# The experts' second product: two passes in place of three for a last block of at most 64 tokens

## What is computed

```python
def _clamped_swiglu(hgu):
    x_glu = jnp.minimum(hgu[..., ::2], SWIGLU_LIMIT)
    x_lin = jnp.clip(hgu[..., 1::2], -SWIGLU_LIMIT, SWIGLU_LIMIT)
    return x_glu * jax.nn.sigmoid(SWIGLU_ALPHA * x_glu) * (x_lin + 1.0)
...
    group_sizes = jnp.bincount(flat_e, length=N_EXPERTS).astype(jnp.int32)
    xs = h[tok]
    hgu = lax.ragged_dot(xs, w_gate_up, group_sizes) + b_gate_up[e_sorted]
    act = _clamped_swiglu(hgu)
    out = lax.ragged_dot(act, w_down, group_sizes) + b_down[e_sorted]
    out = out * gates.reshape(-1)[order][:, None]
    return jax.ops.segment_sum(out, tok, num_segments=L)
```

## Time and profile before

| | us |
|---|---|
| median of 3 executions | 5597.11 |
| lowest and highest | 5595.68 and 5604.63 |
| the profiled execution, its own time | 5600.18 |
| its span in the profile | 5598.8 |
| PE busy / weight loads busy | 5331.9 (95%) / 4757.0 (85%) |
| DVE / ACT / POOL busy | 3565.4 (64%) / 2642.7 (47%) / 614.2 (11%) |
| mean granted clock of TensorE | 0.979 |

### The profile page before, as it was taken

The page is one execution under the profiler, slowest core; times in us unless marked ns, Lnnn a source line. Parts: engine busy times, 40 slices in busy tenths (PEclk is TensorE's granted clock), DMA queues, the critical chain, the costliest instruction groups (busy, mean ns, idle before and its releaser), DMA issues. The chain is left out here.

```text
span 5598.8 us, 92579 instructions
## 1 busy us (share of the span) xinstructions
PE 5331.9 (95%) x30192; PEld 4757.0 (85%) x30193; DVE 3565.4 (64%) x6848; ACT 2642.7 (47%) x5266; POOL 614.2 (11%) x545
## 2 busy tenths in 40 slices
PE   8999979899799999998979999999999999999994
PEld 7777868788799999997869999999899888888894
DVE  6667758533566667776764655655667745577776
ACT  3444331333455556665433534533546534366665
POOL 1101100133000000000220100110101100011113
PEclk9999999999899999999989999999999999999997
DMA  4332335455411101201534744554557644467667
GB/s 145 112 114 92 109 126 166 124 145 152 147 61 59 37 24 61 78 9 57 167 106 132 243 139 166 192 180 146 193 195 234 235 131 157 146 223 246 244 236 251
DMA packets 260439, 809.25 MB, mean 145 GB/s; under 512 B 22305, under 2 KB 168449, under 8 KB 224513
## 3 DMA queue, kind: packets, MB, share of 16 engines
q1 hardware_dynamic: 230352, 717.05, 36.6%
q0 software_dynamic: 27536, 84.88, 6.7%
q10 hardware_dynamic: 2336, 4.45, 0.2%
HBM read 662.84 MB, written 143.47 MB: 144 GB/s over the span
## 5 line engine op out<-in xcount | busy, mean ns | idle before, releaser
L2721 DVE TENSOR_TENSOR e_wl<-r_raw,e_wh 128x1024 fp32r<-128x1024 f32 x770 | 930.1, 1222 | 435.2 <-DVEq L2343 431.8
L2637 ACT CAST e_wh<-r_raw 128x1024 fp32r (+1 forms) x770 | 790.9, 1043 | 864.2 <-ACTq L2343 841.9
L2570 PE MATMUL ps<-e_hT,e_wl 128*128 128x192 f32 (+5 forms) x4096 | 1196.3, 292 | 0.0
L2563 PE MATMUL ps<-e_hT,e_wh 128*128 128x384 f32 (+2 forms) x2560 | 797.2, 374 | 6.1 <-PEq L2343 4.3
L2570 PEld LDWEIGHTS ps<-e_hT,e_wl 128*128 128x128 f32 x4096 | 776.1, 189 | 10.7
L2565 PE MATMUL ps<-e_hT,e_wh 128*128 128x352 f32 (+2 forms) x1536 | 529.4, 345 | 9.0 <-PEq L2343 9.0
L2569 PE MATMUL ps<-e_hT,e_wh 128*128 128x352 f32 (+2 forms) x1536 | 527.2, 343 | 0.0
L2563 PEld LDWEIGHTS ps<-e_hT,e_wh 128*128 128x128 f32 x2560 | 480.3, 188 | 51.6 <-issue 10.7
L2591 PE MATMUL ps<-e_wh,e_aTh 128*128 128x512 f32 x1248 | 504.5, 404 | 5.2 <-PEq L2343 5.2
L1777 ACT CAST a_PT<-ps 128x512 fp32r<-128x512 f32 x512 | 288.0, 589 | 464.7 <-PE ps L1717 464.7
L1732 PE MATMUL ps<-a_PT,a_V 128*128 128x256 f32 (+1 forms) x3264 | 504.3, 294 | 0.2 <-DVE a_sc L1820 0.2
(11 more groups left out here) (367 smaller groups left out, 9329.6 us busy)
## 6 DMA issues: line engine op xcount, KB each, us to landing
r_raw<-in_wgu SPq DMA_DIRECT2D x130, 2048.0 KB
r_raw<-in_wdn SPq DMA_DIRECT2D x64, 2048.0 KB
m_raw<-in_w SPq DMA_DIRECT2D x56, 1024.0 KB, 4.8
qTd<-p_qt SPq DMA_DIRECT2D x32, 640.0 KB, 6.6
e_bd<-in_bdn SPq DMA_DIRECT2D x32, 512.0 KB, 3.8
kTd<-p_kt SPq DMA_DIRECT2D x32, 448.0 KB, 4.3
a_Q<-qTd SPq DMA_DIRECT2D x7, 2048.0 KB, 9.2
a_V<-vd SPq DMA_DIRECT2D x24, 512.0 KB, 4.5
```

The costliest lines, as they stand in the source:

```text
L2563: t = pe.matmul(both, wh, E.hT[:, :, k, 0:v], start=(k == 0), stop=False)
L2570: t = pe.matmul(p[:, 0:v], wl, E.hT[:, 0, k, 0:v], start=False, stop=(k == 7))
L2637: act.copy(E.wh[:, h, x], raw[:, 2048 * h + 1024 * i:2048 * h + 1024 * i + 1024]).then_inc(E.hi_full, 1)
L2721: return dve.tensor_tensor(lo, src, hi.bitcast(F32), ALU.subtract)
```

## The change

`down` is split in two functions. `first` is block 0: its three passes as before, with the low activation's pass ahead of the low weights' one. `later` is a block b >= 1, which now goes pass by pass (4 matmuls of `aTh` by `wh`, 4 of `aTl` by `wh`, 4 of `aTh` by `wl`); the middle pass stands under a branch and is left out when the group's tokens m are at most 128 b + 64, that is, when this is the last block and has at most 64 tokens. For such a group DVE copies the low parts of the last block's first 64 tokens (`aTl`) into the free columns 64 to 127 of that block in `aTh` (`pair`, behind the whole loop of `gate_up` and ahead of the bias), so that one pass over `wh` makes both products, the low one in rows 64 to 127 of the PSUM bank. `outcome` then adds those rows to the first 64 with a second instruction. In every group, short last block or not, PE takes the new semaphore `paired` between block 0 of the stretch (4, 0) and its block 1, and DVE raises it behind the place of the copy. In `outcome` of every block b >= 1 the first instruction is now linked, and `out_full` is raised by a queue instruction behind the branch.

```diff
-    def down(c, h, b, rn):
-        g = product_bank(c, b)
+    def part(g, h, b, k, x, y, start, stop):
+        return pe.matmul(E.G[g][:, :], x[:, 4 * h + k, b * 128:(b + 1) * 128], y[:, h, k * 512:(k + 1) * 512],
+                         start=start, stop=stop)
+
+    def first(c, h, rn):
+        b, g = 0, product_bank(c, 0)
...
-            for m, (x, y) in enumerate(((E.aTh, E.wh), (E.aTh, E.wl), (E.aTl, E.wh))):
...
+            for m, (x, y) in enumerate(((E.aTh, E.wh), (E.aTl, E.wh), (E.aTh, E.wl))):
+                t = part(g, h, b, k, x, y, h == k == m == 0, h == 1 and k == 3 and m == 2)
...
+    def later(c, h, b, rows_here):
+        g = product_bank(c, b)
+        if h == 0:
+            take(pe, E.g_free[g])
+        for k in range(4):
+            part(g, h, b, k, E.aTh, E.wh, h == k == 0, False)
+        with pe.If(rows_here > paired(b)):
+            for k in range(4):
+                part(g, h, b, k, E.aTl, E.wh, False, False)
+        for k in range(4):
+            t = part(g, h, b, k, E.aTh, E.wl, False, h == 1 and k == 3)
+        if h:
+            t.then_inc(E.g_full[g], 1)
...
-            for b in range(4):
-                with present(pe, r, b):
-                    down(c, h, b, rn)
+            first(c, h, rn)
+            if (c, h) == (4, 0):
+                take(pe, E.paired)
+            for b in range(1, 4):
+                with pe.If(r > b):
+                    later(c, h, b, m)
...
+        t = dve.scalar_tensor_tensor(out=E.Y[:, b, cols], in0=E.G[g][:, :], scalar=1.0 / SWIGLU_ALPHA, in1=E.bd[:, cols],
+                                     op0=ALU.mult, op1=ALU.add)
+        if b == 0:
+            t.then_inc(E.out_full[b], 1)
+        else:
+            link(t)
+            with dve.If(rows_here <= paired(b)):
+                link(dve.scalar_tensor_tensor(out=E.Y[0:64, b, cols], in0=E.G[g][64:128, :], scalar=1.0 / SWIGLU_ALPHA,
+                                              in1=E.Y[0:64, b, cols], op0=ALU.mult, op1=ALU.add))
+            dve.sem_inc(E.out_full[b], 1)
         over(E.g_free[g])
...
+    def pair(blocks, rows_here):
+        with dve.If(dve.snap(blocks * 128 + rows_here * -1, min_val=0, max_val=512) >= 64):
+            over(E.dv)
+            take(dve, E.dv)
+            at = dve.snap(blocks * 128 - 128, min_val=0, max_val=384)
+            link(dve.tensor_copy(E.aTh[:, :, bass.ds(at + 64, 64)], E.aTl[:, :, bass.ds(at, 64)]))
+        dve.sem_inc(E.paired, 1)
...
         by_width(dve, m, gate_up, TAKEN)
+        pair(r, m)
         bias()
```

More of the change, by code:

```diff
@@ L2336, in experts_stage @@
     E.own_in, E.own_full, E.summed = sem("own_in"), sem("own_full"), sem("summed")
-    E.dv, E.warmed = sem("dv"), sem("warmed")
+    E.dv, E.warmed, E.paired = sem("dv"), sem("warmed"), sem("paired")
     return E
@@ L2361, with paired @@
 BOTH = 256
+def paired(b):
+    return 128 * b + 64
 def by_width(eng, m, program, widths):
@@ L2596, in down @@
             t.then_inc(E.g_full[g], 1)
+    def later(c, h, b, rows_here):
[11 more added lines that the diff above has]
+            t.then_inc(E.g_full[g], 1)
     ahead = Ahead(E, pe, "pe")
-    first, _, _ = ahead.group()
+    r0, _, _ = ahead.group()
     for b in range(4):
-        with present(pe, first, b):
+        with present(pe, r0, b):
             rows(b, 0)
@@ L2711, in link @@
         take(dve, E.dv)
-    cell = {s: i for i, s in enumerate([E.raw_free] + E.hT_full + E.hx_free + E.g_free + [E.bd_free])}
+    cell = {s: i for i, s in enumerate([E.raw_free] + E.hT_full + E.hx_free + E.g_free + [E.bd_free, E.dv])}
     def over(s):
@@ L2778, in gate_up, with outcome @@
             dve.reg_mov(slot, now * -1 + 1)
-    def outcome(c, b):
+    def outcome(c, b, rows_here):
         g = product_bank(c, b)
@@ L2808, in experts_dve @@
     with groups(E, dve) as q:
-        left = dve.snap(was, min_val=0, max_val=4)
+        left, left_rows = dve.snap(was, min_val=0, max_val=4), dve.snap(was_rows, min_val=0, max_val=512)
         r, rn, m = ahead.group()
@@ L2812, in experts_dve @@
             with dve.If(left > b):
-                outcome(5, b)
+                outcome(5, b, left_rows)
         over(E.bd_free)
@@ L2825, in experts_dve @@
             with present(dve, r, b):
-                outcome(4, b)
+                outcome(4, b, m)
         for i in range(2):
@@ L2834, in experts_dve @@
         dve.reg_mov(was, r)
+        dve.reg_mov(was_rows, m)
         ahead.move()
-    left = dve.snap(was, min_val=0, max_val=4)
+    left, left_rows = dve.snap(was, min_val=0, max_val=4), dve.snap(was_rows, min_val=0, max_val=512)
     for b in range(4):
         with dve.If(left > b):
-            outcome(5, b)
+            outcome(5, b, left_rows)
 def norm_stage(nc, A, banks, sumd, out, eps, since, ctx):
```

20 lines of the change are left out of this document (9 added, 11 removed).

## The result

| | before | after |
|---|---|---|
| median of the runs | 5596.4 us (4 runs, 5595.44 to 5604.63) | 5802.46 us (4 runs, 5799.17 to 5807.29) |
| profiled execution, its span | 5600.2 us (time) | 5799.17 us, span 5797.8 us |
| experts' stage | 2588 us | 2790 us |
| passes of `aTl` over `wh` | 1248 | 1040 |

The ratio is 1.0366, with an interval of 1.0348 to 1.0383: 206 us slower. The direction was forecast, the size was not; 5802 lies far above the range of 5616 to 5670.

What follows compares the result with a forecast made beforehand. PE was taken to bound the experts' stage, busy for 2569.5 of 2588 us. The terms -47.2 + 36.2 + 45.9 + 4 + 6 + 1 gave +46 us, so 5643 us as median, range 5616 to 5670.

Steps and rivals of the forecast that it cites:

- the links on DVE in other places fall in its idle time: DVE's queue in the experts' stage: the other added links cost nothing, as DVE is idle for 37% of the stage.
- cost nothing by themselves: PE's queue: splitting blocks into passes and the new order in `first` add 0 us, as the queue runs ahead.
- a rival at 0.12: TensorE's clock falls in the new pauses: 7 x 3.4 = 24 us more, 5667 us; chance 0.12.
- the price of a pass: PE's second product: 16 matmuls of 0.227 us saved in each of 13 short-ended groups, 47.2 us.
- the new wait: PE ahead of block 1 of (4, 0): 36.2 us added in 16 long-ended groups, 45.9 in the short-ended ones.
- 4 + 1 us beside them: 4 us for one-block groups waiting for `paired`, 1 us for the longer sum at the last group's end.
- saving and paying come out even: The 13 short-ended groups come out nearly even: 47.2 us saved, 45.9 paid.
- the longer sum: `outcome(5, last)` delays ACT's scale, the next weights and PE's second unit in the following group: 6 us (2 to 10).
- Hidden or cheap: Rival: PE's new wait is hidden or cheap, so the kernel gets faster; near 5580 us needs 1 us pauses; chance 0.03.
- even (0.05): Rival: time within 0.2% (11 us), with pauses of 1.6 and 2.6 us and no cost in successors; chance 0.05.
- pass not skipped: Rival: the branch fails to skip the pass or the copy lies elsewhere, only costs left, +93, 5690 us; chance 0.02.
- PE's idle time in the stage: Sign on PE's timeline: idle time in the experts' stage near 110 us instead of 18.5.

Runs made afterwards that it cites:

- after_lean: The changed kernel with width 432 left out of the forms on DVE and ACT, so DVE's loop has 309 instructions; 5686.79 us (1.0156).
- filled: after_lean with eight matmuls that nobody reads, run by PE into a free bank ahead of each take of `paired`; 5652.52 us (1.0094).
- hybrid_act: late_pair with ACT's order of experiment 6, and all four stretches in two passes where the short block is third or fourth; 5578.51 us (0.9965).
- after_shift: The changed kernel, DVE's loop left at 359 instructions, with 80 never-run memsets under a branch ahead of that loop; 5683.34 us (1.0149).
- before_lean: The kernel before with width 432 left out of the forms on DVE and ACT, so DVE's loop has 264 instructions; 5597.97 us (0.9994).
- experiment 6: ACT makes the next group's first pair of high weights ahead of the scale: on late_pair 5588.36 us (0.9982), on before_lean 5600.9 us (1.0004).
- late_pair: after_lean with two passes only in the last two stretches (c = 5), copies made later, behind low weights; 5587.47 us (0.9977) against the kernel before.

## Why the prediction was wrong

**Where it failed: the code.** The step is the pair of sentences that "the links on DVE in other places fall in its idle time" and that the split and the new order "cost nothing by themselves". No term of the sum, and no rival, asked what 45 more instructions in DVE's loop do by being there: the code stood at nothing without a reason. DVE was idle for 37% of the stage, and that hid what they execute, but not their loading, most of which comes at the one place where DVE is on the path, the start of a group. Measured in the changed kernel itself, by moving it: 119 us of the 206, of which some 40 are the clock behind the pauses that the loading makes. That alone puts it outside the range. The question could have been asked blind, since the stage before loads next to no code (6 packets) and the size of the loop can be counted; the price could not, as no row of the kernel before shows a reload.

**Where it failed in part: the clock.** This was a rival at 0.12, worked out at 24 us for the seven longest pauses alone. It happened, and in more places: 22 times in the second products of the changed kernel and in 17 of 32 pauses of `after_lean`, after idle times from 2.03 us up, when I had taken one pause of 3.1 us without a fall as evidence that shorter ones were safe. One row without a fall was no bound: in the changed kernel the pause at 3580.6 us, 2.4 us long, was not followed by a fall, and the one in group 23, just as long, was. The rows of group 23, ahead of the pause, in it and behind:

```profile
5137.54:5139.90 2.36, 2.20 (x12) 1.50 (x10) 1.82 (x4) 1.36 (x3) 0.00 (x0) 1.00 0.08 35
5139.90:5142.10 2.20, 0.00 (x0) 0.00 (x0) 1.47 (x4) 1.48 (x3) 0.00 (x0) 0.91 0.01 4
5142.10:5149.00 6.90, 6.85 (x24) 5.62 (x25) 2.20 (x6) 2.00 (x2) 2.01 (x2) 0.78 0.97 347
```

Here the clock fell while PE was waiting and stayed down for part of the next 6.9 us. `filled` prices the 17 falls: 34 us by the medians, 25 by the profiled executions, net of what its own matmuls cost. The price of a fall, 1.6 us in group 27 and 2.5 in group 28, is less than the 3.4 I had, which counted 0.6 us for the clock inside the pause, where PE has no work to lose; the number of falls is what was missed. The changed kernel has more of them than `after_lean`, 41, and with the 19 behind its reloads the clock is some 76 of its 206 us, by the estimate above. The Trainium skill, TensorE: Matmul & The Clock Gate, section The HAM clock gate, has it that the gate goes to its lower level after an idle window of a free-running monitor. The trace agrees in so far as pauses of the same length are followed by a fall or by none; which it will be I could not foretell from any row, and that a pause of 2.03 us can be enough is what these runs show, not the page.

**Right: the price of a pass.** 47.2 us for 208 matmuls; `hybrid_act` shows 3.46 to 3.66 a group against 3.63.

**Right: the new wait.** Forecast +36.2 and +45.9, with the passes saved and 4 + 1 us beside them +39.9 for the second product. With the clock held up (`filled`) it is +41.2. By the piece, in `after_lean`: group 22 pays 2.36 where 2.26 was forecast, group 29 3.7 where 3.63 was. The start of block 1 alone is later by 35.9 us in the long-ended groups together and 43.9 in the short-ended ones; in the changed kernel, where it is later by 2.5 to 2.6 in a long-ended group (2.2 in group 18) and by 3.5 to 3.8 in a short-ended one of width 192 (4.65 in group 31), it is 40.7 and 47.5. The copy is 0.43 us, forecast 0.4, and runs in 13 groups, as does the second sum (twice each):

```profile
L2828 DVE CAST e_aTh<-e_aTl x13: 426/426/428, 3019.2 to 5706.6; - x13
...
L2818 DVE SCALAR_TENSOR_TENSOR e_Y<-ps,e_Y x26: 693/694/694, 3039.8 to 5726.1; 64x512 f32<-64x512 f32 x26
```

(ns, least, median and most; first and last start). That saving and paying come out even in the groups the change is for was right, with the clock held up: the 13 together are +0.6 us in `filled`, forecast -1.3. In the changed kernel they are +24.6.

**Right in kind, small in size: the longer sum.** Forecast 6 us (2 to 10) in the groups that follow. Without reloads the first product is +3.4 us in `after_shift` against the kernel before, and +13.4 in `after_lean` against `before_lean`; half of the difference is that `before_lean` itself is 5.1 shorter there. The term held within its bounds or nearly, as far as single executions can tell it. The late second unit is there (5.8 us of idle time in `after_lean`, none in `before_lean`), but experiment 6 shows that taking it away does not make the product shorter.

**The rivals.** Hidden or cheap (0.03), even (0.05) and pass not skipped (0.02) all fell: the 29 pauses average 2.9 us, and 1040 passes are there. Of what was to show the forecast wrong, one came true: the granted clock of the stage was under 1.00. And PE's idle time in the stage, said to be near 110 us, was 190.

**The account.** Measured +206, forecast +46. Reloaded code +119, from `after_shift`, its falls of the clock included. In what is left, +81 (`after_shift`) or +86 (`after_lean`), the clock of the new waits is 25 to 34 (`filled` against `after_lean`), and the rest, some 50 to 60, is what the prediction summed to 46; `filled` itself, with no code reloaded and one fall of the clock, is 50 us above the kernel before of its batch (5652.52 against 5602.09).

**Open.** Which layouts of a loop stay loaded: 264, 295, 309 and 320 instructions did, 360 did not, 314 did in one place and not in another, and 359 likewise. The Trainium skill, Advanced Engine Details and Errata, section ISA Cache, gives 32 KB for engines other than TensorE, in lines of 16 KB; the first agrees with such a reading, the second does not with packets of 8 KB. Open too is what PE waits for at the later units of narrow groups once ACT's order is changed.

## What to carry to other kernels

Before a loop body that spans hundreds of instructions is made longer, look at the instruction queue in the profile, and afterwards look again: here five packets for each pass of DVE's loop and a hole behind its branch were a cost that DVE's busy time does not show, and moving or shortening the code took it away. A new wait of TensorE, where TensorE sets the time, costs its length and, here from 2 us on, often the clock behind it as well, whatever the wait comes from, so price it as a pair. And a saving whose data come late is best taken only where PE arrives late: half the passes without a wait (`late_pair`, 13 us faster) and six groups more where the copy is long done (`hybrid_act`, 20 us faster) beat all of them behind a wait (206 us slower).

## What the hardware showed that was not expected

- DVE's loop of 359 instructions was loaded anew in each of 31 passes, in five packets of 8 KB, with a hole of 2.7 to 7.3 us in DVE's queue. The same body 83 instructions further on was not, and the kernel before's 314 were once they lay 47 further on (+83 us). PE's loop of 925 shows nothing of it.
- TensorE's clock fell after idle times as short as 2.03 us (3386.1 us in `after_lean`), but not after each: 2.03 us at 3653.7 us, the same kernel, had no fall. Eight matmuls that nobody reads, put into each pause, kept it up in all but one.
- Matmuls that compute nothing made a kernel faster: 256 of them, 25 to 34 us.
